# The Mamba core of a two-layer backbone: exponents without tensor_scalars, heads in pairs on TensorE

## What is computed

```python
a_cs = jnp.cumsum(a, axis=-1)
decay_in = jnp.exp(segsum(a))
cb = jnp.einsum('bclgn,bcsgn->bgcls', cc, bc)
y_diag = jnp.einsum('bgcls,bgrcls,bcsgrp->bclgrp', cb, decay_in, x)
...
y_off = jnp.einsum('bclgn,bcgrpn,bgrcl->bclgrp', cc, prev_states, jnp.exp(a_cs))
return (y_diag + y_off).reshape(b, L, G, R, P), final
```

## Time and profile before

| | us |
|---|---|
| three executions | 2206.05, 2209.13, 2209.70 |
| median | 2209.13 |
| profiled execution | 2205.01 |
| its span in the trace | 2203.2 |
| TensorE busy (share) | 2043.4 (93%) |
| VectorE busy | 1347.7 (61%) |
| ScalarE busy | 681.6 (31%) |
| GpSimd busy | 223.4 (10%) |

### The profile page before, as it was taken

How to read it: one execution, slowest core, us unless ns; L and a number is a source line. 1 busy time by engine, 2 the same in 40 slices (tenths; PEclk the granted TensorE clock), 3 DMA queues, 4 the chain that set the end, 5 groups by cost and what they waited for, 6 DMA issues and landing times.

```text
span 2203.2 us, 25300 instructions
## 1 busy us (share of the span) xinstructions
PE 2043.4 (93%) x10136; PEld 1697.3 (77%) x10136; DVE 1347.7 (61%) x1875; ACT 681.6 (31%) x881; POOL 223.4 (10%) x172
## 2 busy tenths in 40 slices
PE   5899999999888889999999999999998877798998
PEld 2688888878777768888887888887787864488998
DVE  6664647687665575554666555567755558855544
ACT  3422222232200232222223222223444324434442
POOL 1000001100033300000110000010000005540001
PEclk9999999999999989999999999999999989989999
DMA  8454426544400244443554444454423412345554
GB/s 313 150 177 146 144 76 207 153 166 133 173 1 1 66 154 152 145 151 99 176 158 163 153 134 134 142 163 154 152 78 111 128 34 76 87 116 171 181 161 138
DMA packets 274446, 298.25 MB, mean 135 GB/s; under 512 B 8896, under 2 KB 249120, under 8 KB 272416
## 3 DMA queue, kind: packets, MB, share of 16 engines
q1 hardware_dynamic: 270640, 285.44, 40.8%
q10 hardware_dynamic: 3696, 11.27, 1.3%
HBM read 290.31 MB, written 6.37 MB: 135 GB/s over the span
## 4 chain that ended last, share of the span: by engine, by line
PE 76%; DVE 12%; DMA 4%; issue 3%; ACT 3%; POOL 1%; SPq 0%; DVEq 0%; ACTq 0%; POOLq 0%
PE banks L1483 23%; PE banks L1484 23%; PE banks L1485 23%; DVE wl L890 2%; PE banks L1714 2%; DMA raw<-in_ffn_out 2%; ACT wh L565 2%; DVE xl L953 1%; DVE xt L945 1%; DMA raw<-in_hy_in_w 1%; PE banks L1786 1%; POOL mm L1466 1%; DVE pp L1094 1%; ACT xh L590 1%; DMA dft<-in_c_dft 1%
## 5 line engine op out<-in xcount | busy, mean ns | idle before, releaser
L1483 PE MATMUL banks<-xh,wh 128*128 128x512 f32 (+1 forms) x2120 | 782.7, 369 | 46.4 <-DVE wl L890 20.8
L1484 PE MATMUL banks<-xl,wh 128*128 128x512 f32 (+1 forms) x2120 | 777.1, 367 | 0.0
L1485 PE MATMUL banks<-xh,wl 128*128 128x512 f32 (+1 forms) x2120 | 776.4, 366 | 0.0
L890 DVE TENSOR_TENSOR wl<-raw,wh 128x2048 fp32r<-128x2048 f32 (+1 forms) x196 | 405.4, 2069 | 335.6 <-ACT wh L565 334.3
L565 ACT ACTIVATE wh<-raw 128x2048 fp32r<-128x2048 f32 (+1 forms) x202 | 351.6, 1741 | 611.7 <-PE banks L1485 522.2
L1483 PEld LDWEIGHTS banks<-xh,wh 128*128 128x128 f32 x2120 | 408.8, 193 | 117.0 <-DVE wl L890 23.5
L1485 PEld LDWEIGHTS banks<-xh,wl 128*128 128x128 f32 x2120 | 407.8, 192 | 63.5
L1484 PEld LDWEIGHTS banks<-xl,wh 128*128 128x128 f32 x2120 | 408.7, 193 | 62.0
L1483 PE MATMUL banks<-gh,wh 128*128 128x512 f32 (+1 forms) x704 | 255.8, 363 | 3.9 <-DVE wl L890 2.6
L1484 PE MATMUL banks<-gl,wh 128*128 128x512 f32 (+1 forms) x704 | 255.2, 362 | 0.0
L1485 PE MATMUL banks<-gh,wl 128*128 128x512 f32 (+1 forms) x704 | 255.1, 362 | 0.0
(11 more groups left out here) (209 smaller groups left out, 1844.4 us busy)
## 6 DMA issues: line engine op xcount, KB each, us to landing
raw<-in_ffn_in SPq DMA_DIRECT2D x88, 1024.0 KB, 5.1
raw<-in_ffn_out SPq DMA_DIRECT2D x64, 704.0 KB, 4.9
ada_rawf<-in_ada_rest SPq DMA_DIRECT2D x60, 512.0 KB, 4.1
ada_rawo<-in_ada_rest SPq DMA_DIRECT2D x48, 512.0 KB, 4.2
raw<-in_mb_in_w SPq DMA_DIRECT2D x24, 1024.0 KB, 5.5
raw<-in_hy_in_w SPq DMA_DIRECT2D x12, 1024.0 KB, 5.3
afb<-decays SPq DMA_DIRECT2D x32, 256.0 KB, 3.1
raw<-in_mb_out_w SPq DMA_DIRECT2D x8, 1024.0 KB, 6.0
```

The lines of the kernel that those rows point to most:

```text
L890: dve.tensor_tensor(wl[n_slot][:, 0:cols], raw[r_slot][:, 0:cols], wh[n_slot][:, 0:cols].bitcast(F32), ALU.subtract).then_inc(w_lo, 1)
L1483: pe.matmul(dst, h, x_hi, start=start, stop=False)
L1484: pe.matmul(dst, h, x_lo, start=False, stop=False)
L1485: return pe.matmul(dst, l_, x_hi, start=False, stop=stop)
```

## The change

The engines' work in the core is reordered, and the exponents are formed in another way.

- A new tile `tkd` holds the difference of the two scalars of each head. An exponent is then one scalar_tensor_tensor, the minimum of (one direction's sums + `tkd`) and the other direction's sums, and the scalar left over is added as the bias of ScalarE's exponential. So the tensor_scalars go, with the wait behind them, and L848 becomes two instructions of half the width, as the bias differs.
- VectorE issues `exponents(h + 2)` behind `products(h)` (the multiply by C); those of the first two heads stand between its two calls of `token_major`.
- TensorE takes heads in pairs: the matmuls of the two heads alternate, and it waits for both heads' `cs_done`, then for both heads' `m_done`. `b_dot_c` and `sum_squares` move from behind the first head of a group to behind the first pair.
- GpSimd's and VectorE's products keep their instructions; there are still two buffers `mm_`.
- `cbx` and `afb` change places in memory, and SyncE loads the first four `afb` once `afscr` is written, no longer after the states are copied. The mask is loaded ahead of the `btok` copies.
- The loops of the core are written out on all engines.

```diff
-def core_groups(eng, group, tail, chain=None, per=0):
-    group(0, 0, True, False, False)
-    group(0, 1, False, True, False)
-    with rolled(eng, GROUPS // 2 - 2, chain, per) as i:
-        group(i + 1, 0, False, True, False)
-        group(i + 1, 1, False, True, False)
...
         mm_ = [core(f"mm{i}", [3 * L]) for i in range(2)]
+        cbx = [core(f"cbx{i}", [3 * L]) for i in range(2)]
         afb = [core(f"afb{i}", [2, L]) for i in range(HPG)]
         dm = [core(f"dm{i}", [2 * P]) for i in range(2)]
-        cbx = [core(f"cbx{i}", [3 * L]) for i in range(2)]
...
             sp.wait_ge(af_st, 32)
-            sp.wait_ge(st_out, GROUPS)
-            for r in range(HPG):
-                sp.dma_start(afb[r][:], afscr[r].partition_broadcast(P)).then_inc(afb_in[r], 16)
-            with sp.Fori(0, GROUPS - 1) as g:
+            for g in range(GROUPS):
                 for r in range(HPG):
-                    sp.wait_ge(d_done, g * HPG + r + 1)
-                    sp.wait_ge(e_done, g * HPG + r + 1)
-                    sp.dma_start(afb[r][:], afscr[g * HPG + HPG + r].partition_broadcast(P)).then_inc(afb_in[r], 16)
+                    if g:
+                        sp.wait_ge(d_done, g * HPG + r - 3)
+                        sp.wait_ge(e_done, g * HPG + r - 3)
+                    sp.dma_start(afb[r][:], afscr[g * HPG + r].partition_broadcast(P)).then_inc(afb_in[r], 16)
...
+            act.dma_start(mask[:].rearrange("p a n -> p (a n)"), t["c_mask"]).then_inc(s_mask, 16)
             for b in range(4):
...
-                    act.activation(ee[r][:].rearrange("p (a n) -> p a n", n=P)[:, 0:4:3, :],
-                                   dm[b][:].rearrange("p (a n) -> p a n", n=P), ACT.Exp).then_inc(e_done, 1)
+                act.activation(ee[r][:, 0:P], d_[:, 0:P], ACT.Exp, bias=tk[:, 0, HEADS + h:HEADS + h + 1])
+                act.activation(ee[r][:, 3 * P:4 * P], d_[:, P:2 * P], ACT.Exp,
+                               bias=tk[:, 1, HEADS + h:HEADS + h + 1]).then_inc(e_done, 1)
...
+            own.mark(dve.tensor_tensor(tkd[:], tk[:, 0:2, 0:HEADS], tk[:, 0:2, HEADS:2 * HEADS], ALU.subtract))
...
-                    own.mark(dve.tensor_scalar(d_[:, 0:P], af[:, 0, 0:P], tks[0][0], None, ALU.add))
-                    own.mark(dve.tensor_scalar(d_[:, P:2 * P], af[:, 1, P:L], tks[1][1], None, ALU.add))
-                    own.sync()
-                    own.mark(dve.scalar_tensor_tensor(d_[:, 0:P], af[:, 1, 0:P], tks[1][0], d_[:, 0:P], ALU.add, ALU.min))
-                    dve.scalar_tensor_tensor(d_[:, P:2 * P], af[:, 0, P:L], tks[0][1], d_[:, P:2 * P],
-                                             ALU.add, ALU.min).then_inc(d_done, 1)
+            def exponents(h):
+                g, r = h // HPG, h % HPG
+                af, d_ = afb[r], dm[h % 2]
+                dve.wait_ge(afb_in[r], 16 * g + 16)
+                if h >= 2:
+                    dve.wait_ge(e_done, h - 1)
+                dve.scalar_tensor_tensor(d_[:, 0:P], af[:, 0, 0:P], tkd[:, 0, h:h + 1], af[:, 1, 0:P], ALU.add, ALU.min)
+                dve.scalar_tensor_tensor(d_[:, P:2 * P], af[:, 0, P:L], tkd[:, 1, h:h + 1], af[:, 1, P:L],
+                                         ALU.add, ALU.min).then_inc(d_done, 1)
...
+            token_major(0, 4)
+            dve.wait_ge(s_mask, 16)
+            own.sync()
+            exponents(0)
+            exponents(1)
+            token_major(8, 2)
+            b_dot_c(0)
+            for h in range(HEADS):
+                products(h)
+                if h + 2 < HEADS:
+                    exponents(h + 2)
+                g, r = h // HPG, h % HPG
+                if r == 1 and g:
+                    gate_y(g)
+                if r == 2 and g + 1 < GROUPS:
+                    b_dot_c(g + 1)
+            gate_y(GROUPS)
...
-                for r in range(HPG):
-                    if r == 1 and g + 1 < GROUPS:
-                        b_dot_c(g + 1)
-                    if r == 1 and g >= 2:
-                        sum_squares(g - 2)
...
+                for p in range(HPG // 2):
+                    pair = []
+                    for r in (2 * p, 2 * p + 1):
+                        h = g * HPG + r
+                        pair.append((r, slice(h * HD, h * HD + HD),
+                                     bank[4 + g % 2][r % 2 * HD:r % 2 * HD + HD, p * L:p * L + L]))
+                    pe.wait_ge(cs_done, g * HPG + 2 * p + 2)
+                    for d in range(2):
+                        for r, hc, y in pair:
+                            pe.matmul(y, ssb[:, d, hc], csx[r][:, d * L:d * L + L], start=d == 0, stop=False)
+                    pe.wait_ge(m_done, g * HPG + 2 * p + 2)
+                    for r, hc, y in pair:
+                        pe.matmul(y, xtok[:, 0, 0, hc], mm_[r % 2][:, 0:256], start=False, stop=False)
...
+                    for r, hc, y in pair:
+                        pe.matmul(y, xtok[:, 1, 1, hc], mm_[r % 2][:, 256:512], start=False, stop=True).then_inc(head_mm, 1)
+                    if p == 0 and g + 1 < GROUPS:
                         b_dot_c(g + 1)
+                    if p == 0 and g >= 2:
+                        sum_squares(g - 2)
```

More of the change, by code:

```diff
@@ L294, in build @@
         tk = sb("tk", [6, 64])
+        tkd = sb("tkd", [2, HEADS])
         ident = small[:, 0:P]
@@ L860, in _ @@
+            square_y(GROUPS)
             split_hi(MBOUT.w, CW, MBOUT.raw % 2, MBOUT.raw // 2 + 1, MBOUT.w)
@@ L1349, in gate_y, with products @@
+            def products(h):
+                g, r = h // HPG, h % HPG
+                dve.wait_ge(ex_done, h + 1)
+                cs = csx[r][:].rearrange("p (d n) -> p d n", d=2)
+                dve.tensor_tensor(cs, cs, csb[:, g, :].unsqueeze(1).to_broadcast([P, 2, L]), ALU.mult).then_inc(cs_done, 1)
+            def gate_y(g):
                 dve.wait_ge(head_mm, g * HPG)
-                if not isinstance(g, int) or g > 1:
+                if g > 1:
                     dve.wait_ge(y_done, g - 1)
```

120 lines of the change are left out of this document (39 added, 81 removed).

## The result

The changed kernel takes **2213.5 us** (median of ten runs, 2208.8 to 2216.8), the kernel before 2207.2 in the same series: ratio 1.0026, 95% interval 1.0015 to 1.0036. It is 6 us slower; the forecast was 2216, from a sum of +6.6 on a base of 2209.1. The profiled execution of the changed kernel has a span of 2212.7 us, 9.5 more than before: 1.0 arises ahead of the stage (VectorE's first step on dts starts at 1768.79 instead of 1767.79), 8.8 in it, and behind it 0.3 is given back.

What follows compares the result with a forecast made beforehand. Bound: each head's chain of exponent, exponential, GpSimd product and TensorE product, VectorE and GpSimd taking turns. Terms of -10.2 us at full clock and +16.8 for clock falls gave +6.6 on 2209.1: 2216 us, 8-in-10 range 2196 to 2228.

Steps and rivals of the forecast that it cites:

- First pair on GpSimd: GpSimd's work on a group's first two heads: 3.9 us plus 0.55 for VectorE's steps in between, 4.45 us.
- The turn at full clock: GpSimd waits while TensorE does a pair's products at 2.4 GHz: 1.56 us, plus 0.08 back to GpSimd.
- the heads don't overlap: Rival: TensorE's passes of a pair run one after another, each turn 0.5 to 0.9 us longer; 2212 to 2219, chance 0.17.
- The wait for the sums: Before the fourth head, GpSimd waits for exponentials behind ScalarE's square, which awaits TensorE's sums: 1.45 us, from the third group.
- The group at full clock: Four heads with TensorE at 2.4 GHz take 13.1 us against 14.13 before.
- full clock throughout: Rival: TensorE stays at 2.4 GHz in the whole stage; 2199 us, 2194 to 2204, chance 0.30.
- The fall: TensorE drops to 1.2 GHz after about 3 us idle in each first pair: 2.4 us a group, seven times, +16.8.
- The first two groups: First group -0.4 us, TensorE at 1.2 GHz as before; second -2.5 at full clock, without a sums wait, before its fall of 2.4.
- The start: Before the first group: GpSimd starts 1.6 us earlier through early exponents, less 0.4 for issuing the mask's DMA ahead of btok copies.
- The sum: All terms of the stage together: -10.2 us at full clock and +16.8 for the falls, result +6.6.
- the three waits: In each group GpSimd waits for TensorE every second head and once for ScalarE: turns 1.56 us, sums 1.45.
- the change does little: Rival: GpSimd and VectorE still exclude each other, 1.2 us more in both pairs; near 2208, chance 0.08.

Runs made afterwards that it cites:

- e9: The changed kernel with pairs and waits kept, but TensorE issuing all passes of one head and then the other's; 2215.5 us, ratio 1.0033.
- e5: The changed kernel with three unused matmuls a group filling TensorE's idle time before the first pair's products, groups 1 to 7; 2199.3 us, ratio 0.9963.
- e12: e5 with ScalarE's square of a group moved behind the fourth head's last exponentials; 2205.0 us, ratio 0.9987.
- e3: The changed kernel with four product buffers instead of two, pairs kept; 2207.4 us, ratio 1.0000.
- e8: The changed kernel with TensorE's products head by head, four product buffers, and ScalarE's square behind the fourth head's exponentials; 2195.3 us, ratio 0.9934.
- e1: The changed kernel with six unused matmuls a group in TensorE's idle time before the first pair's products, groups 1 to 7; 2214.8 us, ratio 1.0028.

## Why the prediction was right, point by point

- **First pair on GpSimd**, forecast 4.45: 4.41 (1887.09 to 1891.50). Right; VectorE's insertions are 0.5 us, as taken.
- **The turn at full clock**, forecast 1.56 + 0.08: GpSimd waits 1.74 from its own end, and TensorE needs 1.52 for both heads. Right, to 0.1 us. But why it is right was only half seen: the rival "the heads don't overlap" charged 0.5 to 0.9 us a turn for passes that run one after another, and e9 shows that GpSimd waits for the first head alone. That part of the rival's price nothing pays; whether the later end of the second head costs something at the sums can't be told from e9, whose clock falls at other places. 0.17 of the chance stood on it.
- **The wait for the sums**, forecast 1.45: 1.35 at full clock (e5), 1.35 to 2.70 in the third to the seventh group with falls, and 1.14 in the last. Right as a term. Incomplete as advice: the prediction says that VectorE's wait for b_dot_c lies beside it, but not that VectorE's multiply needs this very pause (e12).
- **The group at full clock**, forecast 13.1: e5 has 13.20, and 2199.3 us in all, where the rival "full clock throughout" was put at 2199.
- **The fall**, forecast in every group from the second on, 2.4 us each, 16.8 in all: it is in every group. It costs 14.2 us by medians (2213.5 against 2199.3), 2.0 a group in the five groups from 1841.80 to 1917.74 (15.19 against 13.20). Right in kind, a sixth too large, and some 2 us of the 14 lie in the first group, where I had forecast none. The Trainium skill ("TensorE: Matmul & The Clock Gate", HAM oscillation — how this bites in real kernels) describes the pattern; the trace agrees, with 3.1 us idle and 0.50 behind it. e5 shows a remedy, which is to give TensorE something to do.
- **The first two groups**, forecast -0.4 and (with a fall) about -0.1: they came out at +1.74 and +1.46. These are the terms that failed. In the first group I had taken the low clock as it was before and gave the rest a guess. In e5, with the same code there, the group is 0.58 shorter than before, close to the guess; in the changed kernel the clock's second fall at 1822 makes the difference. In the second group GpSimd's two pairs take 4.81 and 4.31 us instead of 4.45 and 3.93, and its two waits 2.09 and 4.17 instead of 1.64 each and 2.4 for the fall. Two steps were wrong there. The clock is at 0.50 from 1832.3 to 1842.6, so it lengthens the first turn, for which I had counted it, by 0.35 us only, and catches the second whole, together with the products with the states (L1822) ahead of it: 1837.09 to 1839.07, 1.98 us where they take 1.08 at full clock. And I had counted 1.45 us less because this group has no wait for the sums; e12 shows that a group without that wait gains 0.31, as VectorE's multiply then meets GpSimd's.
- **The start**, forecast -1.6 and +0.4. Both terms are there: GpSimd starts 0.14 us after VectorE's copy (L1298) ends instead of 1.67, and the first btok copy comes 0.44 later because of the mask's DMA. A third was not foreseen: TensorE's transposes and states behind it took 3.67 and 4.56 us instead of 3.13 and 3.72, at the low clock for longer, 0.8 us. Net -0.45 instead of -1.2. Whether the mask's DMA shifted TensorE into that, or it was this execution's clock, wasn't tried.
- **The sum**: six groups forecast at +1.4 each came out at +0.85, 1.51, 0.68, 1.71, 0.86 and 0.41, 6.0 instead of 8.4; the first two 3.2 instead of -0.5; the start -0.45 instead of -1.2. In the profile that is +8.8 where the steps gave +6.6. That the medians differ by 6.3, near the forecast's 6.6, is thus partly luck: errors of both signs, and single runs of the changed kernel lie 8 us apart. What isn't luck is the mechanism: the three waits are there, and it is the falls that turn a gain into a loss (e5).
- **Rival "the change does little"**, 2208 by exclusion: the mechanism is real and larger than the prediction had it, but in the changed kernel VectorE is busy for 10.9 of 14.7 us a group, and GpSimd's waits give it room. It decides in e3, e8 and e12.

## What to carry to other kernels

Batching work for TensorE behind one wait saves nothing when TensorE isn't the bound, and the idle time that it makes can cost the clock: look in the trace for idle stretches of 2 to 3 us with little on either side, and price what follows them at 1.2 GHz. Before a wait of GpSimd is removed, see which VectorE steps with two SBUF operands run in that pause (their shortest against their longest duration shows it); move one operand to PSUM first, and then take the wait away. An experiment whose time equals its reference is not yet a null result: read the trace for two effects that cancel, as in e1.

## What the runs showed of the hardware

- A matmul of 128x512 in fp32 at full clock is recorded as two passes of 0.45 us (12 in 5.42, 6 in 2.84 us), twice what I had counted.
- TensorE's idle times of 3.1 us in the changed kernel came each with a stretch of 0.50 that lasted 3 to 7 us; those of 1.6 to 2.0 us in the same groups did not. The length of the idle time alone doesn't decide: in e12 one of 1.93 us ahead of 1862.54 was followed by a fall and one of the same length ahead of 1877.11 was not, and after 2.89 us (e5, ahead of 1822.01) and 3.27 us (e3, ahead of 1834.30) the clock stayed at 1.00.
- VectorE's 128x512 multiply beside GpSimd takes 0.68 to 1.76 us with both operands in SBUF and 0.67 to 0.68 with one in PSUM, 32 times each. The Trainium skill ("SBUF — State Buffer", Who interferes with whom) says that a VectorE instruction with at most one SBUF input, outside the modes that use both ports, doesn't contend with GpSimd; the trace agrees.
